# Prompt attention of a two-layer decoder step: scores of six of eight query tiles from split queries and keys, in three rounded products

## The chip, the cores and the metric

One core of a Trainium2 chip runs the whole inference step as one program. The metric is the device time of one execution in microseconds, the median of several runs. Five engines take part: TensorE (products and transposes; its weight loads have a queue of their own in the profile), VectorE, ScalarE, GpSimd and the DMA queues. Each engine works through its own instructions in the order in which they were written, and waits on semaphores where an operand comes from another engine.

## The reference, cut to what matters

The step computes two decoder layers for a prompt of 1024 tokens and eight samples of 8 tokens. The first layer's mixer is sparse attention: an indexer scores all keys for each query, the 256 best are kept, and the eight query heads (in two groups, one key head each) attend to them alone:

```python
def dsa_block(q, qi, wi, q_pos, k_all, v_all, ki_all, topk):
    ...
    _, sel = lax.top_k(score, topk)
    ...
    s = jnp.einsum('bqhgd,bqkhd->bqhgk', q, k_sel) * (HEAD_DIM ** -0.5)
    s = jnp.where(sel_valid[:, :, None, None, :], s, -jnp.inf)
    p = jax.nn.softmax(s, axis=-1)
    o = jnp.einsum('bqhgk,bqkhd->bqhgd', p, v_sel)
```

Everything is float32. What the change touches is the first `einsum`, for the prompt: head by head, 128 queries against the keys before them.

## The kernel before, in words

The program runs stage by stage: load, indexer projections, indexer scores, search of the 256th score together with the query, key and value projections, attention of the samples, **attention of the prompt** (`prompt_attention_stage`, lines 3547 to 3793), output projection, then the feed-forward, gated and second feed-forward stages, which take most of the time (702 us to the end).

The prompt attention keeps queries and keys, transposed, in `proj` (128 rows of a head by 1088 tokens; tiles `QT` to `QT + 7` are the query heads, `KTILE` and `KTILE + 1` the key heads), values in `v_nat`, and a mask per query tile in `mp`, which is 0 where a key was selected and very negative elsewhere. A query tile i has 128 queries and (i + 1) x 128 keys. The work is 64 steps, one per tile and head, in an order written out by hand: tile 0, tile 2, tile 3 (steps 0 to 23, a head at a time), then tiles 1 and 4 in turns (steps 24 to 39), then tiles 5, 6, 7 (steps 40 to 63).

A step s goes through the engines like this:

- TensorE, `scores` (line 3628): queries of the tile by the keys, in pieces of up to 512 columns, into one of two score banks. It needs `tops` of step s - 2 to be done.
- VectorE, `tops` (line 3737): adds the mask, negates, and takes the row's minimum, all in one instruction (line 3745) of the tile's whole width.
- ScalarE, `exps` (line 3690): the exponential with that minimum as bias, and the row's sum.
- VectorE: the reciprocal of the sum (line 3768).
- TensorE, `turn_probs` (line 3644): transposes the probabilities, 128 columns at a time, into two banks that ScalarE (line 3715, even groups) and VectorE (line 3764, odd groups) copy out.
- TensorE, `values` (line 3655): the product with the values; `scale_out` (ScalarE, line 3703, up to step 40, then VectorE, line 3749) divides by the sum; TensorE `turn_out` (line 3638) transposes and ScalarE `copy_out` (line 3698) writes the result over the step's queries in `proj`.

The order within one turn of the loops sets what overlaps. TensorE does `turn_probs(s)`, `values(s - 1)`, `turn_out(s - 2)`, `scores(s + 2)`. ScalarE does its copies of s, `exps(s + 1)`, `scale_out(s - 1)`, `copy_out(s - 2)`. VectorE does `tops(s + 1)`, its copies of s, the reciprocal of s, from step 41 `scale_out(s - 1)`. At the end of a turn both have other work at chosen steps: a search that lowers a threshold bit by bit for the last two tiles (`late.compare`, line 2489, on VectorE, and `late.add`, line 2496, on ScalarE, at steps 16, 18, 20, 22, 23 and every second step from 25 to 37), and the masks of tiles 4 to 7 (`masks.step`, lines 2562 to 2577, on VectorE at steps 8 to 10, 12 to 14, 40 to 42, 44 to 46; `masks.write`, line 2581, on ScalarE). From step 58 five heads' results are split for the next stage's rounded products: a copy into `hi` (line 3726) on ScalarE, and `value - hi` (line 3789) on VectorE a step later.

A float32 product appears in the trace as two matmul records with two weight loads; a transpose as one. Products of operands of type `F32R` (rounded float32) appear as one record. The other stages use such rounded products already, three in place of one: high by high, high by low, low by high. In the indexer scores it is two (lines 2939 and 2940) with the halves stacked.

The buffers of this stage lie in an arena that begins where `proj` begins, in slots of 1088 columns: `x_lo` at slot 0 lies on the query heads, `x_hi` at slot 12; slots 10 and 11 (`VTILE`) are free in this stage.

Of the kernel before, what the change touches and what calls it, by code (L numbers as in the profile page):

```python
# [20 lines left out]
F32 = mybir.dt.float32  # L21
F32R = mybir.dt.float32r
BF16 = mybir.dt.bfloat16
I32 = mybir.dt.int32
ALU = mybir.AluOpType
# [3 lines left out]
P = 128  # L29
D = 1024  # L30
KT = D // P
SEQ = 1024
# [3511 lines left out]
SPLIT_HEADS = 5  # L3544


def prompt_attention_stage(nc, proj, v_nat, Sp, level, mp, last_level, xT, x_kept, v_outs, x_parts, nxt, g):


    steps = [(i, h) for i in (0, 2, 3) for h in range(NH)]  # L3550
# [14 lines left out]
    with Scope(nc, "patt") as S:  # L3565
# [10 lines left out]
        copied = [S.sem("copied0"), S.sem("copied1")]  # L3576
        x_loaded, v_stored = S.sem("x_loaded"), S.sem("v_stored")
        hi, lo = x_parts
        out_hi, out_lo = S.sem("out_hi"), S.sem("out_lo")
        finished = {starts[7] + h + 2: h for h in range(SPLIT_HEADS)}  # L3580
        NR = len(SP_TILES)
# [44 lines left out]
        @block.tensor  # L3626
        def _(pe):
            def scores(s):
                i, h = steps[s]
                if s >= 2:  # L3630
                    pe.wait_ge(ntop_ready, s - 1)
                for a in range(0, width(s), 512):
                    w = min(512, width(s) - a)
                    last = nc.tensor.matmul(sc[s % 2][:, a:a + w], proj[:, QT + h, i * P:(i + 1) * P],
                                            proj[:, KTILE + h // GR, a:a + w], start=True, stop=True)
                last.then_inc(scored, 1)

            def turn_out(s):
                wait_scaled(pe, s)
                if s >= 1:  # L3640
                    pe.wait_ge(o_copied, s)
                nc.tensor.transpose(o_tr[:, 0:P], o_rows[:, s % 2, :], g["ident"][:, :]).then_inc(o_turned, 1)

            def turn_probs(s):
                pe.wait_ge(exp_ready, s + 1)
                for j in of_step[s]:
                    _, a, n = groups[j]
                    if j >= 2:
                        wait_copied(pe, j - 2)
                    for t in range(n):  # L3650
                        last = nc.tensor.transpose(tr[j % 2][:, t * P:(t + 1) * P], prob[:, s % 2, (a + t) * P:(a + t + 1) * P],
                                                   g["ident"][:, :])
                    last.then_inc(turned, 1)

            def values(s):
                i, h = steps[s]
                for j in of_step[s]:
                    wait_copied(pe, j)
                if s:
                    wait_scaled(pe, s - 1)  # L3660
                kv = h // GR
                for t in range(i + 1):
                    last = nc.tensor.matmul(out[:, 0:HD], probT[:, s % 2, t * P:(t + 1) * P],
                                            v_nat[:, t, kv * HD:(kv + 1) * HD], start=(t == 0), stop=(t == i))
                last.then_inc(pv_ready, 1)

            scores(0)
            scores(1)
            for s in range(n_steps):
                turn_probs(s)  # L3670
                if s:
                    values(s - 1)
                if s >= 2:
                    turn_out(s - 2)
                if s + 2 < n_steps:
                    scores(s + 2)
            values(n_steps - 1)
            for s in (n_steps - 2, n_steps - 1):
                turn_out(s)
# [9 lines left out]
        def _(act):  # L3689
# [22 lines left out]
            for s in range(n_steps):  # L3712
                for j in of_step[s]:
                    if j % 2 == 0:
                        copy_group(act, j, lambda o, i: nc.scalar.activation(o, i, ACT.Copy))
                if s + 1 < n_steps:
                    exps(s + 1)
                if 1 <= s <= by_act:
                    scale_out(s - 1)
                if s >= 2:  # L3720
                    copy_out(s - 2)
                if s in finished:
                    h = finished[s]
                    act.wait_ge(o_copied, s - 1)
                    act.wait_ge(masks.written, NR - MASKED)
                    nc.scalar.activation(hi[:, h, :], proj[:, QT + h, :], ACT.Copy).then_inc(out_hi, 1)
                if s in round_at:
                    late.add(nc, act, round_at[s])
                if s in mask_after:
                    masks.write(nc, act, mask_after[s])  # L3730
# [5 lines left out]
        def _(dve):  # L3736
# [22 lines left out]
            for s in range(n_steps):  # L3759
# [23 lines left out]
                    late.settle_level(nc, dve)  # L3783
                if s in tails:
                    masks.step(nc, dve, *tails[s])
                if s - 1 in finished:
                    h = finished[s - 1]
                    dve.wait_ge(out_hi, h + 1)
# [374 lines left out]
def trunk(nc, a, o):  # L4163
    with Scope(nc, "trunk") as T, nc.allow_non_contiguous_dma(reason="a few small vectors and 8 x 8 blocks"):
# [38 lines left out]
        with Scope(nc, "att") as A:  # L4203
# [21 lines left out]
            with Scope(nc, "masks") as C:  # L4225
# [21 lines left out]
                first = {n: Next(T, W, n, t, True, {"sgout": 1}.get(n, 2))  # L4247
                         for n, t in (("attout", attout), ("ffn0", ffn[0]), ("sgin", sgin), ("sgout", sgout), ("ffn1", ffn[1]))}
                x_parts = arena.at(T, "x_hi", [P, KT, TOK], F32R, 12), arena.at(T, "x_lo", [P, KT, TOK], F32R, 0)
                prompt_attention_stage(nc, proj, v_nat, Sp, level, mp, last_level, xT, x_kept, v_outs, x_parts, first["attout"], g)  # L4250
            ahead = [arena.at(T, f"x_ahead{i}", [P, len(AHEAD), TOK], F32R, 20) for i in range(2)]
            x_low = arena.at(T, "x_low", [P, 20, TOK], F32R, 0)
            with Scope(nc, "attoutx") as X:
# [43 lines left out]
```

## Time and profile before

| | us |
|---|---|
| median of 3 runs | 2587.63 (2586.83 to 2588.19) |
| the profiled execution, its time | 2604.05 |
| its span in the trace | 2602.3 |
| prompt attention, first score to last `copy_out` | 521.3 to 702.2 |
| busy over the span: TensorE | 2481.4 (95%) |
| VectorE | 1823.3 (70%) |
| ScalarE | 1150.1 (44%) |
| scores of the stage (line 3634): records, and time in them | 192, 77 us |

Times of instructions are those of one profiled execution. Instructions of TensorE overlap: a record lasts longer than the distance to the next one, so what a product costs is read from the distance between the starts or the ends of neighbours, not from its duration. On VectorE and ScalarE neighbours overlap by some 0.1 us. PEclk is the clock granted to TensorE, as a share of 2.4 GHz. "[0.58 <-ACT patt_prob]" at the end of a row is the engine's idle time before the instruction, and what ended it.

### The profile page before, as it was taken

The page shows a single profiled execution, that of the slowest core. Times are in us where ns is not written, and L with a number is a line of the kernel's source. Part 1 is how long each engine was busy: PE and PEld are TensorE (multiplying, and loading weights), DVE is VectorE, ACT ScalarE, POOL GpSimd, SP SyncE. Part 2 cuts the span into 40 slices and gives each one's busy share as a digit, 9 for nine tenths or more (in the row PEclk, how much of TensorE's full clock was granted, in tenths as well). Part 3 has the DMA queues.
Part 4 walks back from the last instruction along what each step waited for, and adds up shares of the span by engine and source line. Part 5 has one row for each costly group of instructions (what it writes and reads, how often), then busy time and mean ns, then how long its engine had stood idle before and what let it go on. Part 6 is the DMA issues. An engine that isn't in the chain of part 4 may idle for free. (4 is left out here: it accounts for less than half of the span.)

```text
span 2602.3 us, 49502 instructions
## 1 busy us (share of the span) xinstructions
PE 2481.4 (95%) x19001; PEld 2369.4 (91%) x19032; DVE 1823.3 (70%) x3373; ACT 1150.1 (44%) x1956; POOL 107.2 (4%) x135
## 2 busy tenths in 40 slices
PE   8899988899999999999999999989999999999898
PEld 7799955567899999999998999989999999999898
DVE  6658776777557888886575676664788888656652
ACT  5567686576534333342331353553443343323121
POOL 1310033200000000000000000000000000000000
PEclk9889999999999999999999999999999999999999
DMA  6312379820022343442775323234144433268522
GB/s 207 86 50 70 116 290 370 345 103 1 18 100 67 135 143 134 145 140 97 273 260 191 112 74 109 68 90 168 56 138 145 156 143 134 91 234 286 212 78 81
DMA packets 276591, 371.91 MB, mean 143 GB/s; under 512 B 22152, under 2 KB 215946, under 8 KB 268237
## 3 DMA queue, kind: packets, MB, share of 16 engines
q1 hardware_dynamic: 264573, 294.23, 33.2%
q0 software_dynamic: 11776, 75.50, 7.8%
q8 instruction: 101, 1.65, 0.3%
q14 instruction: 61, 0.50, 0.1%
q10 hardware_dynamic: 80, 0.02, 0.0%
HBM read 271.07 MB, written 98.63 MB: 142 GB/s over the span
## 5 line engine op out<-in xcount | busy, mean ns | idle before, releaser
L1542 PE MATMUL ffn_acc<-trunk_x_ahead,trunk_w_hi 128*128 128x272 f32 x2464 | 470.5, 290 | 5.0 <-ACT ffn_t_u L949 3.9
L1542 PE MATMUL ffn_acc<-ffn_x_later,ffn_w_hi_more 128*128 128x272 f32 x2112 | 396.4, 287 | 1.5 <-DVE trunk_xT L1190 1.5
L1542 PEld LDWEIGHTS ffn_acc<-trunk_x_ahead,trunk_w_hi 128*128 128x128 f32 x2464 | 389.0, 190 | 5.4 <-issue 5.4
L1542 PE MATMUL ffn_acc<-trunk_x_ahead,trunk_w_lo 128*128 128x272 f32 x1232 | 355.8, 289 | 0.0
L1542 PEld LDWEIGHTS ffn_acc<-ffn_x_later,ffn_w_hi_more 128*128 128x128 f32 x2112 | 330.8, 188 | 1.8 <-issue 1.8
L1542 PE MATMUL ffn_acc<-ffn_x_later,ffn_w_lo_more 128*128 128x272 f32 x1056 | 303.8, 288 | 0.0
L1542 PEld LDWEIGHTS ffn_acc<-trunk_x_ahead,trunk_w_lo 128*128 128x128 f32 x1232 | 233.7, 190 | 0.0
L1542 PEld LDWEIGHTS ffn_acc<-ffn_x_later,ffn_w_lo_more 128*128 128x128 f32 x1056 | 198.8, 188 | 0.0
L1595 PE MATMUL ffn_acc<-trunk_x_ahead,trunk_w_hi 128*128 128x272 f32 x896 | 175.2, 293 | 14.4 <-DVE trunk_xT L1415 14.1
L1595 PE MATMUL ffn_acc<-ffn_x_later,ffn_w_hi_more 128*128 128x272 f32 x768 | 149.0, 291 | 12.8 <-DVE trunk_xT L1415 6.9
L1595 PEld LDWEIGHTS ffn_acc<-trunk_x_ahead,trunk_w_hi 128*128 128x128 f32 x896 | 143.8, 193 | 15.6 <-issue 11.2
L920 ACT ACTIVATE ffn_w_hi_more<-trunk_w_raw 128x512 fp32r<-128x512 f32 x132 | 83.4, 632 | 167.8 <-PE ffn_acc L1542 163.9
L1415 DVE TENSOR_TENSOR trunk_xT<-ffn_acc,trunk_xT 128x544 f32<-128x544 f32 x136 | 98.2, 722 | 77.4 <-PE ffn_acc L1595 76.8
L920 ACT ACTIVATE trunk_w_hi<-ffn_w_sum 128x512 fp32r<-128x512 f32 x88 | 55.6, 632 | 206.7 <-DVE ffn_w_sum L1171 115.6
L1619 PE MATMUL ffn_acc<-trunk_x_ahead,trunk_w_hi 128*128 128x364 f32 (+1 forms) x576 | 141.8, 327 | 0.0
L1595 PEld LDWEIGHTS ffn_acc<-ffn_x_later,ffn_w_hi_more 128*128 128x128 f32 x768 | 122.5, 192 | 14.3 <-DVE trunk_w_lo L1404 7.7
L1595 PE MATMUL ffn_acc<-trunk_x_ahead,trunk_w_lo 128*128 128x272 f32 x448 | 130.7, 292 | 0.0
L3304 PE MATMUL search_acc<-attxm_x_pairs,attxm_w_hi 128*128 128x364 f32 (+1 forms) x480 | 122.1, 336 | 1.9 <-PEq L87 1.9
L1595 PE MATMUL ffn_acc<-ffn_x_later,ffn_w_lo_more 128*128 128x272 f32 x384 | 111.9, 291 | 0.0
L1005 ACT ACTIVATE trunk_xT<-trunk_xT 128x544 fp32r<-128x544 f32 x112 | 71.7, 655 | 90.5 <-DVE trunk_xT L1249 48.8
L1190 DVE TENSOR_TENSOR trunk_xT<-ffn_acc,ffn_u 128x544 f32<-128x544 f32 x88 | 63.6, 722 | 63.2 <-PE ffn_acc L1542 63.2
L1619 PEld LDWEIGHTS ffn_acc<-trunk_x_ahead,trunk_w_hi 128*128 128x128 f32 x576 | 101.6, 188 | 0.0
(525 smaller groups left out, 6084.6 us busy)
## 6 DMA issues: line engine op xcount, KB each, us to landing
o_kept<-trunk_xT SPq DMA_DIRECT2D x96, 544.0 KB, 5.0
trunk_w_raw<-in_ffn_w_gu SPq DMA_DIRECT2D x88, 512.0 KB, 4.0
trunk_x_ahead<-o_kept SPq DMA_DIRECT2D x56, 544.0 KB, 7.5
ffn_x_later<-o_kept SPq DMA_DIRECT2D x56, 544.0 KB, 7.6
x_saved<-trunk_xT SPq DMA_DIRECT2D x24, 544.0 KB, 2.7
trunk_w_raw<-in_ffn_w_down SPq DMA_DIRECT2D x48, 192.0 KB, 4.0
o_kept<-trunk_xT SPq DMA_DIRECT2D x32, 272.0 KB, 4.9
ffn_x_back<-x_saved SPq DMA_DIRECT2D x16, 544.0 KB, 5.8
```

The costliest lines, as they stand in the source:

```text
L920: nc.scalar.activation(w_parts(i)[0], source, ACT.Copy).then_inc(w_hi_ready, 1)
L1005: nc.scalar.activation(stage_hi[STAGE_OF[i][0]], raw_block[i], ACT.Copy).then_inc(kept_hi, 1)
L1190: nc.vector.tensor_tensor(two(out), pair(b), two(a), ALU.add).then_inc(done, 1)
L1415: nc.vector.tensor_tensor(two(out), pair(bank_of(z, n)), two(out), ALU.add).then_inc(d_added, 1)
L1542: last = nc.tensor.matmul(bank(2 * PAIR[p] + c)[:, 0:QC], w[:, k * P:(k + 1) * P], x(p, k)[:, c * QC:(c + 1) * QC], start=FRESH[p] and k = ...
L1595: last = nc.tensor.matmul(bank(2 * bank_of(z, n) + c)[:, 0:QC], w[:, k * P:(k + 1) * P], x(i, at)[:, c * QC:(c + 1) * QC], start=n in (0, ...
L1619: last = nc.tensor.matmul(bank(NC3 * (q % 2) + c)[:, 0:w], part[:, q % 2, k * P:(k + 1) * P], x[:, a:a + w], start=(k == 0 and j == 0), st ...
L3304: last = nc.tensor.matmul(banks[NC3 * (m % 2) + c][:, 0:w], part[:, k * P:(k + 1) * P], x_parts[x][:, k, a:a + w], start=(k == 0 and j == ...
```

## The change

For tiles 1, 3, 4, 5, 6 and 7 the scores are no longer one float32 product but three rounded ones into the same bank: high part of the queries by high part of the keys, high by low, low by high. Tiles 0 and 2 stay as they were.

The parts are made in this stage. A high part is a copy to type `F32R` on ScalarE, a low part is the difference to it, on VectorE. Keys are split in two halves of 512 tokens, both heads at once (128 x 2 x 512), at steps 1 and 5; the queries of a tile, all eight heads at once (128 x 8 x 128), at steps 3 (tile 3), 15 (tile 1), 17 (tile 4), 29 (tile 5), 43 (tile 6) and 47 (tile 7). Both come at the end of the step's turn on their engine, ScalarE's ahead of `late.add`, VectorE's behind `late.compare` and the masks. The low parts of the queries are written in place, over the queries; high parts have three buffers that are used in turn; `k_hi` lies in slots 10 and 11.

```diff
@@ -3544,7 +3544,7 @@
 SPLIT_HEADS = 5
 
 
-def prompt_attention_stage(nc, proj, v_nat, Sp, level, mp, last_level, xT, x_kept, v_outs, x_parts, nxt, g):
+def prompt_attention_stage(nc, proj, v_nat, Sp, level, mp, last_level, xT, x_kept, v_outs, x_parts, k_hi, nxt, g):
 
 
     steps = [(i, h) for i in (0, 2, 3) for h in range(NH)]
@@ -3576,6 +3576,14 @@
         copied = [S.sem("copied0"), S.sem("copied1")]
         x_loaded, v_stored = S.sem("x_loaded"), S.sem("v_stored")
         hi, lo = x_parts
+        split_tiles = (3, 1, 4, 5, 6, 7)
+        q_hi, k_lo = S.sb("q_hi", [P, 3, NH, P], F32R), S.sb("k_lo", [P, NKV, SEQ], F32R)
+        q_hi_ready, q_lo_ready, k_hi_ready, k_lo_ready = (S.sem(n) for n in ("q_hi_ready", "q_lo_ready", "k_hi_ready", "k_lo_ready"))
+        k_split_at, q_split_at = {1: 0, 5: 1}, {3: 0, 15: 1, 17: 2, 29: 3, 43: 4, 47: 5}
+        last_step = lambda i: max(s for s, x in enumerate(steps) if x[0] == i)
+        queries = lambda n: proj[:, QT:QT + NH, split_tiles[n] * P:(split_tiles[n] + 1) * P]
+        queries_lo = lambda n: lo[:, :, split_tiles[n] * P:(split_tiles[n] + 1) * P]
+        half_of = lambda v, e: v[:, :, 512 * e:512 * (e + 1)]
         out_hi, out_lo = S.sem("out_hi"), S.sem("out_lo")
         finished = {starts[7] + h + 2: h for h in range(SPLIT_HEADS)}
         NR = len(SP_TILES)
@@ -3629,10 +3637,21 @@
                 i, h = steps[s]
                 if s >= 2:
                     pe.wait_ge(ntop_ready, s - 1)
+                kv = h // GR
+                if i in split_tiles:
+                    n = split_tiles.index(i)
+                    pe.wait_ge(q_lo_ready, n + 1)
+                    pe.wait_ge(k_lo_ready, 1 if width(s) <= 512 else 2)
                 for a in range(0, width(s), 512):
                     w = min(512, width(s) - a)
-                    last = nc.tensor.matmul(sc[s % 2][:, a:a + w], proj[:, QT + h, i * P:(i + 1) * P],
-                                            proj[:, KTILE + h // GR, a:a + w], start=True, stop=True)
+                    if i in split_tiles:
+                        q_high, q_low = q_hi[:, n % 3, h, :], lo[:, QT + h, i * P:(i + 1) * P]
+                        for j, (q, k) in enumerate(((q_high, k_hi[:, kv, a:a + w]), (q_high, k_lo[:, kv, a:a + w]),
+                                                    (q_low, k_hi[:, kv, a:a + w]))):
+                            last = nc.tensor.matmul(sc[s % 2][:, a:a + w], q, k, start=j == 0, stop=j == 2)
+                    else:
+                        last = nc.tensor.matmul(sc[s % 2][:, a:a + w], proj[:, QT + h, i * P:(i + 1) * P],
+                                                proj[:, KTILE + kv, a:a + w], start=True, stop=True)
                 last.then_inc(scored, 1)
 
             def turn_out(s):
@@ -3719,6 +3738,14 @@
                     scale_out(s - 1)
                 if s >= 2:
                     copy_out(s - 2)
+                if s in k_split_at:
+                    e = k_split_at[s]
+                    nc.scalar.activation(half_of(k_hi, e), half_of(proj[:, KTILE:KTILE + NKV, :], e), ACT.Copy).then_inc(k_hi_ready, 1)
+                if s in q_split_at:
+                    n = q_split_at[s]
+                    if n >= 3:
+                        act.wait_ge(scored, last_step(split_tiles[n - 3]) + 1)
+                    nc.scalar.activation(q_hi[:, n % 3, :, :], queries(n), ACT.Copy).then_inc(q_hi_ready, 1)
                 if s in finished:
                     h = finished[s]
                     act.wait_ge(o_copied, s - 1)
@@ -3783,6 +3810,16 @@
                     late.settle_level(nc, dve)
                 if s in tails:
                     masks.step(nc, dve, *tails[s])
+                if s in k_split_at:
+                    e = k_split_at[s]
+                    dve.wait_ge(k_hi_ready, e + 1)
+                    nc.vector.tensor_tensor(half_of(k_lo, e), half_of(proj[:, KTILE:KTILE + NKV, :], e),
+                                            half_of(k_hi, e).bitcast(F32), ALU.subtract).then_inc(k_lo_ready, 1)
+                if s in q_split_at:
+                    n = q_split_at[s]
+                    dve.wait_ge(q_hi_ready, n + 1)
+                    nc.vector.tensor_tensor(queries_lo(n), queries(n), q_hi[:, n % 3, :, :].bitcast(F32),
+                                            ALU.subtract).then_inc(q_lo_ready, 1)
                 if s - 1 in finished:
                     h = finished[s - 1]
                     dve.wait_ge(out_hi, h + 1)
@@ -4247,7 +4284,9 @@
                 first = {n: Next(T, W, n, t, True, {"sgout": 1}.get(n, 2))
                          for n, t in (("attout", attout), ("ffn0", ffn[0]), ("sgin", sgin), ("sgout", sgout), ("ffn1", ffn[1]))}
                 x_parts = arena.at(T, "x_hi", [P, KT, TOK], F32R, 12), arena.at(T, "x_lo", [P, KT, TOK], F32R, 0)
-                prompt_attention_stage(nc, proj, v_nat, Sp, level, mp, last_level, xT, x_kept, v_outs, x_parts, first["attout"], g)
+                k_hi = arena.at(T, "k_hi", [P, NKV, TOK], F32R, VTILE)
+                prompt_attention_stage(nc, proj, v_nat, Sp, level, mp, last_level, xT, x_kept, v_outs, x_parts, k_hi, first["attout"],
+                                       g)
             ahead = [arena.at(T, f"x_ahead{i}", [P, len(AHEAD), TOK], F32R, 20) for i in range(2)]
             x_low = arena.at(T, "x_low", [P, 20, TOK], F32R, 0)
             with Scope(nc, "attoutx") as X:
```

## Rows read from the trace of the kernel before

**Rows 1.** Busy time by stretch of 15 us: PE, PEld, DVE, ACT, POOL, PEclk, DMA share, GB/s.

```profile
575.00:590.00 15.00, 13.86 (x95) 10.98 (x95) 11.15 (x41) 13.08 (x39) 0.00 (x0) 1.00 0.01 2
...
650.00:665.00 15.00, 15.00 (x103) 12.14 (x102) 8.09 (x20) 8.03 (x16) 0.00 (x0) 1.00 0.01 1
```

**Rows 2.** TensorE in order of time, tiles 6 and 7: start us, us, engine, line, operation.

```profile
656.25 1.67 PE L3634 MATMUL patt_sc<-att_proj 128*128 128x512 f32 x4
657.75 0.93 PE L3651 MATMUL patt_tr<-trunk_ident,patt_prob 128*128 128x128 f32 x7
...
660.19 1.88 PE L3634 MATMUL patt_sc<-att_proj 128*128 128x512 f32 x4
661.91 0.93 PE L3651 MATMUL patt_tr<-trunk_ident,patt_prob 128*128 128x128 f32 x7
```

**Rows 3.** TensorE in order of time, indexer scores with rounded operands, at full clock.

```profile
88.11 0.39 PE L2939 MATMUL sel_banks<-idx_k_hi,idx_q 128*128 128x512 f32 x1
...
88.58 1.00 PE L2986 MATMUL sel_banks<-att_proj 128*128 128x64 f32 x8
...
93.73 0.31 PE L2939 MATMUL sel_banks<-idx_k_hi,idx_q 128*128 128x128 f32 x1
93.88 0.27 PE L2940 MATMUL sel_banks<-idx_k_lo,idx_q 128*128 128x128 f32 x1
...
111.38 0.37 PE L2939 MATMUL sel_banks<-idx_k_hi,idx_q 128*128 128x256 f32 x1
111.59 0.28 PE L2940 MATMUL sel_banks<-idx_k_lo,idx_q 128*128 128x256 f32 x1
...
123.87 0.42 PE L2939 MATMUL sel_banks<-idx_k_hi,idx_q 128*128 128x384 f32 x1
124.13 0.34 PE L2940 MATMUL sel_banks<-idx_k_lo,idx_q 128*128 128x384 f32 x1
```

**Rows 4.** Groups of instructions by form: splits of 128x1024 elsewhere (count, busy us, mean ns).

```profile
L295 DVE TENSOR_TENSOR trunk_w_lo<-trunk_w_raw,trunk_w_hi 128x1024 fp32r<-128x1024 f32 x1 | 1.2, 1217 | 0.0
...
L291 ACT ACTIVATE trunk_w_hi<-trunk_w_raw 128x1024 fp32r<-128x1024 f32 x1 | 1.1, 1051 | 0.0
```

**Rows 5.** In order of time, all engines, tile 0 (first steps of the stage).

```profile
524.69 0.37 ACT L3708 ACTIVATE patt_o_rows<-patt_out,patt_rtotal 128x128 f32<-128x128 f32 x1 [0.60 <-PE patt_out L3663]
...
525.12 0.29 DVE L3745 CUSTOM_DVE_ANT_0 patt_prob<-patt_sc,masks_mp 128x128 f32<-128x128 f32 x1 [0.49 <-PE patt_sc L3634]
...
527.63 0.27 ACT L3701 ACTIVATE att_proj<-patt_o_tr 128x128 f32<-128x128 f32 x1
527.67 0.29 DVE L3745 CUSTOM_DVE_ANT_0 patt_prob<-patt_sc,masks_mp 128x128 f32<-128x128 f32 x1 [0.45 <-PE patt_sc L3634]
```

**Rows 6.** Busy time by stretch of 1 us, start of the stage.

```profile
524.00:525.00 1.00, 1.00 (x6) 0.89 (x5) 0.36 (x2) 0.40 (x2) 0.00 (x0) 0.50 1.08 304
```

**Rows 7.** In order of time, steps 14 to 18, tile 2 into tile 3.

```profile
548.60 0.69 DVE L3745 CUSTOM_DVE_ANT_0 patt_prob<-patt_sc,masks_mp 128x512 f32<-128x512 f32 x1 [0.33 <-PE patt_sc L3634]
...
548.87 0.26 ACT L3701 ACTIVATE att_proj<-patt_o_tr 128x128 f32<-128x128 f32 x1
...
550.90 0.60 PE L3651 MATMUL patt_tr<-trunk_ident,patt_prob 128*128 128x128 f32 x4
...
553.40 0.69 DVE L3745 CUSTOM_DVE_ANT_0 patt_prob<-patt_sc,masks_mp 128x512 f32<-128x512 f32 x1 [0.93 <-PE patt_sc L3634]
```

**Rows 8.** In order of time, tiles 1 and 4, around step 29.

```profile
581.93 0.82 DVE L3745 CUSTOM_DVE_ANT_0 patt_prob<-patt_sc,masks_mp 128x640 f32<-128x640 f32 x1
...
583.76 0.77 PE L3651 MATMUL patt_tr<-trunk_ident,patt_prob 128*128 128x128 f32 x5 [0.58 <-ACT patt_prob L3695]
```

**Rows 9.** In order of time, tile 5 and the start of tile 6.

```profile
619.78 0.27 ACT L3701 ACTIVATE att_proj<-patt_o_tr 128x128 f32<-128x128 f32 x1
...
620.11 0.96 DVE L3745 CUSTOM_DVE_ANT_0 patt_prob<-patt_sc,masks_mp 128x768 f32<-128x768 f32 x1 [1.05 <-PE patt_sc L3634]
...
634.20 1.09 DVE L3745 CUSTOM_DVE_ANT_0 patt_prob<-patt_sc,masks_mp 128x896 f32<-128x896 f32 x1 [0.92 <-PE patt_sc L3634]
```

## The prediction

> **What bounds the kernel now.** The change touches one stage, the prompt attention, 521.3 to 702 us of the trace. I read first how busy each engine is by stretch, to see who could be the limit. In the long tiles TensorE has no free time and the other two are little over half busy [rows 1]; where tiles 1 and 4 alternate, TensorE has over 1 us free in 15 while ScalarE is busy 13.1 of 15 [rows 1]. So there are two kinds of stretch: TensorE-bound ones (most of tile 3, the end of tile 5, tiles 6 and 7), where cheaper scores are time, and ones bound by a loop through VectorE (`tops`), ScalarE (`exps`) and TensorE (turning the probabilities), where they are not. Next I read TensorE in order of time for what scores cost [rows 2], and the indexer's scores, the nearest work with rounded operands [rows 3]; last, ScalarE and VectorE in order of time at the eight steps where splits are put in [rows 5, 7, 8, 9].
>
> **Scores.** A full-precision product shows as two records. In tile 7 the scores (2 x 512 columns) start at 660.19 and the next transposes at 661.91: 1.72 us, 0.86 per 512 columns. In tile 6 (512 + 384) it is 1.50 us, so 0.64 for 384 [rows 2]; at the same rate per column 256 cost 0.43 and 128 cost 0.215. A rounded pass is one record. Two of 512 columns take 88.11 to 88.58, 0.235 each; 384, by the ends (124.29 and 124.47), 0.18; 256 (111.75 and 111.87) 0.12; 128 (94.04 and 94.15) 0.11 [rows 3]. Three passes: 0.70, 0.54, 0.36, 0.33. So 512 columns save 0.16, 384 save 0.10, 256 save 0.07, and 128 *lose* 0.11, since a pass that short is as long as its weight load. Per step: tile 7 0.32, tile 6 0.26, tile 5 0.23, tile 3 0.16, tile 1 0.07, tile 4 0.05; times 8 heads, 8.7 us of TensorE time in all. TensorE's clock is full in both groups of rows.
>
> The rows say 0.70 against 0.86, which is 0.82. The Trainium skill (FP8 and Floating Point Precision, TensorE Precision Notes) says that true FP32 takes four passes through the array; three for four would be 0.75, 0.65 us for 512 columns, and 8 x (0.43 + 0.38 + 0.32 + 0.27 + 0.22 + 0.11), some 13.8 us, instead of 8.7. The rows decide, and no run here yet shows these three passes themselves.
>
> **What of it reaches the end.** Tiles 1 and 4: nothing. TensorE waits for an exponential before each tile-4 step (0.58 us at 583.76 [rows 8]), and its own scores are not in that loop. Tile 3: TensorE sets the pace there from step 17 to 22; of the five scores in between, the first two fall before the second of my stalls below, so 3 x 0.16 = 0.5. Tile 5: VectorE is full there with the masks of tiles 6 and 7, and one step's 0.2 counts. Tiles 6 and 7: five steps x 0.26 and eight x 0.32, 3.9. Together **-4.6 us**.
>
> **The splits.** Eight pairs: two for the keys (steps 1, 5), six for queries (3, 15, 17, 29, 43, 47). Each is a 128x1024 copy on ScalarE and a 128x1024 subtraction on VectorE; the nearest rows are 1.05 and 1.22 us [rows 4]. In work that is 8.4 and 9.8 us on engines with time to spare. But the order decides. In a step, ScalarE does the exponential of step s+1, the scaling, the copy out, and then the rounding; VectorE waits for it at the end of the same step, and behind that wait stands `tops` of s+2, for which the next exponential waits, and for that TensorE. So `tops` starts at ScalarE's end of the step + 1.05 + 1.22 instead of when its scores are there.
> - Step 1: ScalarE is done at 524.69 + 0.37 = 525.06, so the subtraction ends at 527.33; `tops` began at 525.12 [rows 5]: 2.2 late. TensorE, at half clock there [rows 6], was a few tenths behind; I take 1.7.
> - Step 3: done at 527.90, so 530.17 against 527.67 [rows 5]: 2.5, with nothing to hide it.
> - Step 5: the same pattern, 2.2. Scores that TensorE does meanwhile give back 0.5. Tile 0 together: +5.9.
> - Step 15: done at 549.13, so 551.40 against 548.60: 2.8. Then 1.6 for `tops` and exponential: 553.0, against TensorE's next turn at 550.90 [rows 7]. I take +2.0.
> - Step 17: all is 2.0 later by now, and ScalarE also does one of the search's additions every second step, so that I estimate the end of its step at 555.7. With 2.3 for the pair `tops`, at 553.40 before [rows 7], comes at 558.0: 4.6 late, 2.6 more than what came over from step 15, of which I take 0.6 for TensorE's margin. Another +2.0.
> - Step 29: VectorE is full until 581.93 [rows 8], by when the copy is done; only the 1.2 of the subtraction count, and TensorE waited there already: +1.2.
> - Steps 43, 47: ScalarE is done with 43 at 619.78 + 0.27 = 620.05, so the subtraction ends at 622.3 against 620.11, where VectorE had waited 1.05 for scores [rows 9]: 2.2 late, of which about 1.2 stay, since VectorE's masks of the next steps leave it no other gap. At 47 the same comes on top: `tops`, at 634.20 before [rows 9], would start at 637.9, 3.7 late. In a step of 3.94 us (656.25 to 660.19 [rows 2]) `tops` (1.09) and the exponential (some 1.2) leave TensorE 1.7 of margin: together +2.0.
>
> Sum: 5.9 + 2.0 + 2.0 + 1.2 + 2.0 = **+13.1 us**. Bounds of each: 0 if the engine ahead has the slack, and the full 2.3 of the pair of instructions. The waits that the change gives TensorE (low parts ready) are met many steps before. The wait for a query buffer at 29, 43 and 47 is for scores of steps 23, 38 and 39, done by then. No DMA is added or moved.
>
> **The clock.** TensorE's granted clock is 0.50 (the 1.2 GHz level) at 524 [rows 6], after the thin work between the two stages. With three stalls of some 2 us in tile 0 TensorE is again thinly used, and I expect part of tiles 0 and 2 at the lower level. A step of tile 0 has six 128-column records of 0.11, 0.66 us at full clock; about half of them lie in the loop, so half clock costs some 0.3 us a step. Five steps of that: **+1.5**. Bounds: nothing, and 4 us if the first steps of tile 2, with three times the products, also run at half clock.
>
> **Sum.** -4.6 + 13.1 + 1.5 = +10.0. The profiled execution took 2604.05 us (span 2602.3), 0.6% over the median of 2587.63; the differences are in microseconds of one stage and carry over: 2614 for a profiled execution, **2597** for the median (I shade the sum down by half a microsecond, since every stall was taken alone). The stage behind starts from TensorE's last transposes, so what is lost here stays lost. A measurement of this kernel can tell about 0.2%, 5.2 us.
>
> **Rivals.**
> - *Faster: the stalls are hidden.* If the copy and the subtraction slip into idle time what is left is TensorE's gain on the TensorE-bound steps: 5 x 0.16, 6 x 0.23, 8 x 0.26 and 8 x 0.32, 6.8 in all, so 2581. For: in tiles 6 and 7 both engines have 7 of 15 us free [rows 1]. Against: only two of the eight splits come near those tiles, and rows 5 and 7 show `tops` starting as soon as its scores are there, so that whatever stands before it is late work. It decides if `tops` behind a split starts less than 0.5 us late. 0.14.
> - *No change: half hidden.* The stalls of tile 0 shrink because engines run ahead in the gaps, steps 43 and 47 are absorbed by TensorE's margin, and the clock is as before: 3 + 3 + 1 - 5 = +2, 2590. 0.25.
> - *Slower by more: the clock.* If TensorE stays at half clock from 524 through the first steps of tile 2, 1.5 becomes 4 to 5 and stalls add to each other: 2601. For: the fall at 524 after thin work. Against: it was back within some 3 us. It decides at the granted clock of 530 to 540. 0.15, beside 0.46 for the forecast itself; both are slower, 0.61.
> - *The change doesn't do what it says:* if a rounded pass issued as two records, scores would cost half more. The 44 rounded indexer products have 44 records, so under 0.01.
>
> **Numbers.** Faster by over 0.2% (below 2582.4) 0.14; within 0.25; slower (above 2592.8) 0.61. Range 2583 to 2603: the lower end leaves out the fully hidden case, the upper end is the bad clock with full stalls.
>
> **What the profile after would show.** (1) Scores of tile 7 take about 1.40 us before the transposes, not 1.72; one record per pass. (2) Behind each of steps 1, 3, 5, 15 and 17, VectorE idle for about 1 us waiting for ScalarE's rounding copy, then TensorE idle about 2 us for an exponential. (3) Tile 0 takes about 15 us, not 9. (4) No gain in tiles 1 and 4; tiles 6 and 7 4 us shorter. (5) A granted clock of 0.5 within 527 to 540. I am wrong if VectorE's wait for the copy is short, if the transposes behind a split don't wait, or if the passes interleave to less than 0.23 us for 512 columns.

## The result, and the profile after

| | before | after |
|---|---|---|
| median of 9 runs each, one chip, us | 2588.19 (2586.83 to 2594.66) | 2596.61 (2591.68 to 2600.47) |
| ratio, 95% interval | | 1.003 (1.002 to 1.0041) |
| prompt attention, first score to the first product of the output projection, us | 181.2 | 190.3 |
| where that stage starts in the trace, us | 521.3 | 507.3 |

The kernel is slower by 8.4 us. The forecast was 2597 on a median of 2587.63, 9.4 more; its sum was +10.0. The profiled execution after is shorter in all (2593.72 us, span 2591.9) than the one before: its prompt attention starts 14 us earlier, since the stages ahead of it, which the change doesn't touch, took less time in that execution. So everything below compares the stage alone: 190.3 against 181.2, 9.1 us longer.

To see where, take the first transposes of each step, counted from those of step 0, in both traces. The difference is the delay that the change has built up by that step (us; the other columns are the experiments below):

| step | after | E1 | E2 | E3 | E4 | E5 | E6 | E8 |
|---|---|---|---|---|---|---|---|---|
| 3 | 1.65 | -0.09 | 1.65 | -0.01 | 0.07 | -0.01 | 1.65 | 0.00 |
| 5 | 4.11 | 1.06 | 4.12 | 0.45 | 1.04 | 0.45 | 3.81 | 0.00 |
| 7 | 6.37 | 2.02 | 6.38 | 0.57 | 1.55 | 0.58 | 5.77 | 0.00 |
| 16 | 6.39 | 2.39 | 6.40 | 0.58 | 1.58 | 3.96 | 5.79 | 0.00 |
| 17 | 8.33 | 2.80 | 8.34 | 0.48 | 1.99 | 3.86 | 7.73 | -0.09 |
| 19 | 10.07 | 3.02 | 10.08 | 0.33 | 2.20 | 3.72 | 9.47 | -0.24 |
| 25 | 9.86 | 3.13 | 10.16 | -0.11 | 1.91 | 5.50 | 9.27 | -0.68 |
| 33 | 11.28 | 3.50 | 11.59 | -0.10 | 2.00 | 5.50 | 11.39 | -0.61 |
| 40 | 11.29 | 3.51 | 11.61 | -0.08 | 2.04 | 7.91 | 11.36 | -0.53 |
| 49 | 13.06 | 4.12 | 13.63 | -0.61 | 1.50 | 9.43 | 13.14 | -1.04 |
| 56 | 11.08 | 2.07 | 13.68 | -2.66 | -0.54 | 7.39 | 11.14 | -3.08 |
| 63 | 9.13 | 0.10 | 13.69 | -4.62 | -2.50 | 5.44 | 9.20 | -5.05 |

All engines in order of time, tile 0 of the kernel after, steps 1 and 3 (rows of other lines left out). These answer to [rows 5].

```profile
510.93 1.05 ACT L3743 ACTIVATE trunk_k_hi<-att_proj 128x1024 fp32r<-128x1024 f32 x1
...
512.01 1.23 DVE L3816 TENSOR_TENSOR patt_k_lo<-att_proj,trunk_k_hi 128x1024 fp32r<-128x1024 f32 x1 [1.41 <-ACT trunk_k_hi L3743]
...
513.15 0.28 DVE L3772 CUSTOM_DVE_ANT_0 patt_prob<-patt_sc,masks_mp 128x128 f32<-128x128 f32 x1
...
514.03 0.47 PE L3670 MATMUL patt_tr<-trunk_ident,patt_prob 128*128 128x128 f32 x1 [1.45 <-ACT patt_prob L3714]
...
515.59 1.06 ACT L3748 ACTIVATE patt_q_hi<-att_proj 128x1024 fp32r<-128x1024 f32 x1
...
516.68 1.23 DVE L3821 TENSOR_TENSOR trunk_x_lo<-att_proj,patt_q_hi 128x1024 fp32r<-128x1024 f32 x1 [1.78 <-ACT patt_q_hi L3748]
...
518.70 0.48 PE L3670 MATMUL patt_tr<-trunk_ident,patt_prob 128*128 128x128 f32 x1 [1.60 <-ACT patt_prob L3714]
```

Read it as one chain: VectorE idles 1.41 us until ScalarE's copy is done, subtracts for 1.2, and only then does `tops` (513.15), whose scores were there some 2 us before; the exponential follows, and TensorE has idled 1.45 us when it comes. The same chain at steps 15 and 29, where [rows 7] and [rows 8] were:

```profile
541.39 1.05 ACT L3748 ACTIVATE patt_q_hi<-att_proj 128x1024 fp32r<-128x1024 f32 x1
542.48 1.23 DVE L3821 TENSOR_TENSOR trunk_x_lo<-att_proj,patt_q_hi 128x1024 fp32r<-128x1024 f32 x1 [1.83 <-ACT patt_q_hi L3748]
...
545.21 0.66 PE L3670 MATMUL patt_tr<-trunk_ident,patt_prob 128*128 128x128 f32 x4 [1.94 <-ACT patt_prob L3714]
...
576.61 1.06 ACT L3748 ACTIVATE patt_q_hi<-att_proj 128x1024 fp32r<-128x1024 f32 x1
...
577.76 1.22 DVE L3821 TENSOR_TENSOR trunk_x_lo<-att_proj,patt_q_hi 128x1024 fp32r<-128x1024 f32 x1
...
580.73 0.77 PE L3670 MATMUL patt_tr<-trunk_ident,patt_prob 128*128 128x128 f32 x5 [1.87 <-ACT patt_prob L3714]
```

At step 29 the subtraction has no bracket: VectorE was full until 577.8, and the copy had ended at 577.67, just in time. Over the stage, the waits sum up so (line waited for: us, times, longest):

```profile
PE patt_tr L3670 <- ACT patt_prob L3714: 20.4, 24, 1.9
DVE patt_prob L3772 <- PE patt_sc L3651: 13.2, 15, 1.3
...
DVE trunk_x_lo L3821 <- ACT patt_q_hi L3748: 9.8, 5, 2.1
...
DVE patt_k_lo L3816 <- ACT trunk_k_hi L3743: 3.2, 2, 1.8
```

TensorE waited for an exponential 6.8 us in the stage before (14 times) and now 20.4. VectorE waits 13.0 us for copies, seven times (at step 29 it doesn't), and correspondingly less for scores: 13.2 us for rounded ones and 2.1 for float32 ones, where it had been 29.7. Its wait changed its place from ahead of a `tops` whose scores weren't there to ahead of one whose scores were.

TensorE in order of time, scores of tile 7 after, answering to [rows 2]:

```profile
667.06 1.03 PE L3670 MATMUL patt_tr<-trunk_ident,patt_prob 128*128 128x128 f32 x8
...
669.75 0.48 PE L3651 MATMUL patt_sc<-trunk_k_hi,patt_q_hi 128*128 128x512 f32 x1
670.07 0.40 PE L3651 MATMUL patt_sc<-patt_k_lo,patt_q_hi 128*128 128x512 f32 x1
670.31 0.40 PE L3651 MATMUL patt_sc<-trunk_k_hi,trunk_x_lo 128*128 128x512 f32 x1
670.54 0.39 PE L3651 MATMUL patt_sc<-trunk_k_hi,patt_q_hi 128*128 128x512 f32 x1
670.77 0.39 PE L3651 MATMUL patt_sc<-patt_k_lo,patt_q_hi 128*128 128x512 f32 x1
671.00 0.39 PE L3651 MATMUL patt_sc<-trunk_k_hi,trunk_x_lo 128*128 128x512 f32 x1
671.23 1.03 PE L3670 MATMUL patt_tr<-trunk_ident,patt_prob 128*128 128x128 f32 x8
```

One record per pass, and from 670.07 to 671.23 five passes in 1.16 us, 0.232 each, so six take 1.39. The first starts 0.32 ahead of the second, in the shadow of a transpose that began at 669.72. The step is 671.23 - 667.06 = 4.17 us; the same step before was 4.49.

Busy time by stretch of 1 us at the start of the stage (PE, PEld, DVE, ACT, POOL, PEclk, DMA share, GB/s), answering to [rows 6]:

```profile
509.00:510.00 1.00, 0.48 (x4) 0.29 (x4) 0.30 (x2) 0.98 (x5) 0.00 (x0) 0.56 1.08 314
...
517.00:518.00 1.00, 0.09 (x1) 0.00 (x0) 1.00 (x2) 0.00 (x0) 0.00 (x0) 0.50 1.00 405
...
522.00:523.00 1.00, 0.62 (x1) 0.00 (x0) 1.00 (x5) 0.17 (x1) 0.00 (x0) 0.61 1.02 402
523.00:524.00 1.00, 0.62 (x3) 0.46 (x4) 0.58 (x4) 1.00 (x5) 0.00 (x0) 1.00 1.05 376
```

The granted clock is 0.50 (1.2 GHz) in every microsecond between. By the shares in the first and the last of them it stood there for 13.7 us, from 1.8 to 15.5 us into the stage; before, for 3.4 us, from 2.5 to 5.9 us into it. VectorE alone at work for a whole microsecond (517) is the stall.

### The profile page after: what moved, and what is told of

It reads as the page before. It is cut to its first block and busy times, and to the rows that moved or that the text cites. A ratio compares the mean times of both kernels' runs of the same rounds, so it can differ in the third digit from the quotient of the medians.

```text
span 2591.9 us, 49730 instructions
## 1 busy us (share of the span) xinstructions
PE 2466.5 (95%) x19081; PEld 2374.9 (92%) x19112; DVE 1829.7 (71%) x3381; ACT 1156.9 (45%) x1964; POOL 108.2 (4%) x135
## 5 line engine op out<-in xcount | busy, mean ns | idle before, releaser
L1595 PEld LDWEIGHTS ffn_acc<-trunk_x_ahead,trunk_w_hi 128*128 128x128 f32 x896 | 143.0, 192 | 17.6 <-issue 13.2
```

Of the source, the lines that this page charges most:

```text
L1595: last = nc.tensor.matmul(bank(2 * bank_of(z, n) + c)[:, 0:QC], w[:, k * P:(k + 1) * P], x(i, at)[:, c * QC:(c + 1) * QC], start=n in (0, ...
```

## Experiments

The theory after this: the eight pairs cost 13.7 us (the 9.1, and the 4.6 that the passes were to give), and they cost it as *waits in a fixed order* (copy, subtraction, then `tops`), hardly as work; the passes give 4.6; the low clock adds something. Rivals: the work itself is what costs; the passes give more or less than their share in the last tiles; the clock is most of tile 0. Diffs are against the changed kernel.

**E1, the subtraction a step later.** The same work, but VectorE no longer waits for a copy of its own step.

```diff
-                if s in k_split_at:
-                    e = k_split_at[s]
+                if s - 1 in k_split_at:
+                    e = k_split_at[s - 1]
...
-                if s in q_split_at:
-                    n = q_split_at[s]
+                if s - 1 in q_split_at:
+                    n = q_split_at[s - 1]
```

> Each of the eight subtractions moved one step later on VectorE, nothing else changed. The stage (first score to the first product of the output projection) took 181.2 us before and 190.3 after the change. Order theory (VectorE's wait for ScalarE's copy holds up tops): the wait goes, ScalarE's 1.05 and VectorE's 1.2 stay but now lie beside each other's slack; each split costs about 1.2 instead of 1.2 to 2.1, tile 0 is 3 to 3.5 us longer than before instead of 6.2, the stage 184 to 186, the kernel 2590 to 2593. Work theory (the copies and subtractions cost what they are long, wherever they stand): the stage stays at 189.5 to 190.5, the kernel at 2596 to 2597.

Measured: 2587.16 us (2584.13 to 2590.17, 11 runs), kernel before on that chip 2589.35; ratio 0.9993 (0.9983 to 1.0003). The stage took 181.3 us, 0.1 more than before the change and 2.7 below the lower end of what I expected. In order of time, step 3:

```profile
513.15 1.05 ACT L3748 ACTIVATE patt_q_hi<-att_proj 128x1024 fp32r<-128x1024 f32 x1
...
514.24 1.23 DVE L3821 TENSOR_TENSOR trunk_x_lo<-att_proj,patt_q_hi 128x1024 fp32r<-128x1024 f32 x1 [0.82 <-ACT patt_q_hi L3748]
514.80 0.33 PE L3670 MATMUL patt_tr<-trunk_ident,patt_prob 128*128 128x128 f32 x1 [0.78 <-ACT patt_prob L3714]
...
515.38 0.28 DVE L3772 CUSTOM_DVE_ANT_0 patt_prob<-patt_sc,masks_mp 128x128 f32<-128x128 f32 x1
```

The copy runs while VectorE does the `tops` that the next exponential needs; `tops` after next waits instead, which is less urgent. All of the change's loss is gone with the same instructions: 9.1 - 0.1 = 9.0 us were order. That includes what the order did to the clock, which was at 0.50 for only 3.4 us here, as before the change; E6 below puts a price on it. At step 49 the column stands at 4.1: what the work of the splits costs (2.4 in tile 0, where a step is shorter than the pair), less the little that the passes gave until there. In tiles 6 and 7 the passes give 4.0 back. At steps 15 and 17 the pairs cost 0.6 together instead of 3.7.

**E2, the splits alone.** All eight pairs stay, and every score is one float32 product again (with the low part of the queries, which lies where they were; their values are left out).

```diff
-                if i in split_tiles:
+                if i in ():
...
-                        last = nc.tensor.matmul(sc[s % 2][:, a:a + w], proj[:, QT + h, i * P:(i + 1) * P],
+                        q = lo[:, QT + h, i * P:(i + 1) * P].bitcast(F32) if i in split_tiles else proj[:, QT + h, i * P:(i + 1) * P]
+                        last = nc.tensor.matmul(sc[s % 2][:, a:a + w], q,
```

> All splits as in the changed kernel, but the scores are one float32 product as before (for the six tiles with the low part of the queries, so their values are left out). If the passes give what the rows said (4.6 us on the path), the stage is 190.3 + 4.9 = 195 us and the kernel 2601; if the passes give nothing and the splits cost 9, the stage is 190 to 191 and the kernel 2597.

Measured: 2602.74 us (5 runs), ratio 1.0052 (1.0039 to 1.0065); the stage 194.9. The E2 column follows that of after to step 19 and then lacks only what the passes give: 0.3 at 25, 0.6 at 49, and 13.69 - 9.13 = 4.6 at the end. From step 25 to 40 both columns rise by 1.4, so in tiles 1 and 4 the passes gave nothing.

**E3, the passes alone.** No splits; the parts are buffers of zeros, filled by GpSimd at the start, so queries and keys are left out of these scores.

```diff
+        @block.gpsimd
+        def _(pool):
+            for t in (q_hi[:, :, :, :], k_lo[:, :, :], k_hi[:, :, :]):
+                nc.gpsimd.memset(t.bitcast(F32), 0.0).then_inc(q_lo_ready, 1)
...
-                    pe.wait_ge(q_lo_ready, n + 1)
+                    pe.wait_ge(q_lo_ready, 3)
...
-                        q_high, q_low = q_hi[:, n % 3, h, :], lo[:, QT + h, i * P:(i + 1) * P]
+                        q_high = q_low = q_hi[:, n % 3, h, :]
```

> Three rounded passes, no splits: the parts are zeroed once by GpSimd and the masks alone then decide (the split of queries and keys is left out). My sum: TensorE's gain on its own steps, 5 to 7 us: stage 174 to 176, kernel 2581 to 2583. If a pass is dearer than in the indexer's rows: stage 178 or more.

Measured: 2582.87 us (7 runs), ratio 0.9975 (0.9964 to 0.9985); the stage 176.5, 4.6 under the kernel before and 0.5 over the upper end of what I expected from it. Its column has 0.57 at step 7, where no score has changed yet: the granted clock was 0.50 for 6.8 us here, not 3.4. In E8, whose first steps are the same for TensorE, it was 3.4 and the column shows 0.00, so the 0.57 is the clock's. Behind that E3's column falls by 0.7 to step 25, by 0.5 from 40 to 49 and by 4.0 in tiles 6 and 7. E2 and E3 add up, 13.7 - 4.6 = 9.1, but in part by luck: the 4.6 is 5.2 of passes less 0.6 of clock, and alone the passes give 0.7 in tile 3 where beside the splits they gave 0.3.

**E5, both parts on GpSimd.** The copy and the subtraction leave ScalarE and VectorE altogether.

```diff
+        @block.gpsimd
+        def _(pool):
...
+                    nc.gpsimd.tensor_copy(q_hi[:, n % 3, :, :], queries(n)).then_inc(q_hi_ready, 1)
...
+                    nc.gpsimd.tensor_tensor(queries_lo(n), queries(n), q_hi[:, n % 3, :, :].bitcast(F32),
+                                            ALU.subtract).then_inc(q_lo_ready, 1)
```

> Copy and subtraction of all eight splits on GpSimd, at the same steps' semaphores but with no place in ScalarE's and VectorE's order. Order theory and work theory both: what they lose is given back unless GpSimd is late or slows VectorE: stage 174 to 177, kernel 2581 to 2584. Rival: GpSimd takes so long for 128x1024 (over 5 us for a pair) that the first scores of tile 3 wait, or VectorE's instructions get longer beside it: stage 180 or more.

Measured: 2591.06 us (12 runs), ratio 1.0006 (0.9997 to 1.0015); the stage 186.6, ten more than my theory allowed: the rival was right. GpSimd and VectorE in order of time:

```profile
523.33 0.78 DVE L2564 TENSOR_SCALAR patt_tail_eq<-masks_Sp,masks_level 128x640 bf16<-128x640 f32 x1
...
523.85 2.50 POOL L3649 TENSOR_TENSOR trunk_x_lo<-att_proj,patt_q_hi 128x1024 fp32r<-128x1024 f32 x1
...
525.10 2.59 DVE L2570 TENSOR_TENSOR_SCAN patt_rank<-patt_tail_eq 128x640 f32<-128x640 bf16 x1
...
526.30 2.23 POOL L3647 CAST patt_q_hi<-att_proj 128x1024 fp32r<-128x1024 f32 x1
...
528.61 2.81 POOL L3649 TENSOR_TENSOR trunk_x_lo<-att_proj,patt_q_hi 128x1024 fp32r<-128x1024 f32 x1
...
529.24 2.52 DVE L2577 TENSOR_TENSOR patt_tail_hit<-patt_tail_hit,patt_tail_eq 128x640 bf16<-128x640 bf16 x1
...
556.00 2.37 POOL L3649 TENSOR_TENSOR trunk_x_lo<-att_proj,patt_q_hi 128x1024 fp32r<-128x1024 f32 x1
...
556.17 2.22 DVE L2512 SCALAR_TENSOR_TENSOR masks_last_level<-masks_last_level,patt_late_drop 128x2 int32<-128x2 int32 x1
...
558.42 1.15 ACT L2496 ACTIVATE patt_late_hit<-masks_Sp,masks_last_level 128x1024 bf16<-128x1024 f32 x1 [1.38 <-DVE masks_last_level L2512]
```

A VectorE instruction of two numbers a partition takes 2.22 us and ends at 558.39, when GpSimd's subtraction ends (558.37); undisturbed it is 0.16. The mask's sum takes 2.52, to the end of GpSimd's at 531.4 and its own 0.49 less an overlap. It works the other way too: GpSimd's copy, 1.04 elsewhere, takes 2.23 and ends 0.84 behind VectorE's scan. `tops`, which reads its scores from PSUM, and the copies out of PSUM kept their times, which is why the pairs in tile 0 cost nothing (E5 and E3 are equal to step 7). Two inputs in SBUF are no condition, though: the mask's comparison (line 2564), with one, took 0.78 and not 0.55, and one of the search's on two numbers (line 2510), also with one, 0.95 and not 0.17. The delay comes at once from step 8 to 16 (+3.4) and between 19 and 25 (+1.8), with the masks and the search. Of the +3.9 between 33 and 49 the search accounts for 2.3, at step 39. The next 1.8 came at step 41 with GpSimd at rest: TensorE had stood idle for 2.4 us ahead of step 39, and from 600.9 to 607.7 its granted clock was 0.50. The Trainium skill (SBUF — State Buffer, Who interferes with whom) says that VectorE and GpSimd share one pair of SBUF ports, that it is an exclusive lock, and that a VectorE instruction with two SBUF inputs contends with a GpSimd instruction that reads SBUF; the times above agree with that.

**E6, TensorE kept busy in tile 0.** Three 128-column products ahead of the transposes of steps 2 to 7, in an unused part of a score bank.

```diff
+                if 2 <= s < 8:
+                    for _ in range(3):
+                        nc.tensor.matmul(sc[0][:, 512:512 + P], g["ident"][:, :], g["ident"][:, :], start=True, stop=True)
```

> The changed kernel, with three float32 products of 128 columns (six records, 0.66 us at full clock) that nobody reads put ahead of each step's transposes in steps 2 to 7, into a score bank that is free then. After the change TensorE's clock stood at 0.50 for 13 us (509.5 to 522.5). If that clock costs what I had put down for it (1.5 us), it comes back some us earlier here and the eighth step's transposes come at 6.2 - 1 to 6.2 + 0.5 us beyond before (the products themselves lie in the stalls); the 2.2 us of each split stay. If the clock, not VectorE's order, were the cause of tile 0's 6.2 us, they would fall to 3 or less.

Measured: one execution, 2601.43 us; the stage 190.4, that of after 190.3. Stretches of 1 us, same columns as above:

```profile
515.00:516.00 1.00, 1.00 (x7) 1.00 (x6) 0.42 (x1) 0.55 (x1) 0.00 (x0) 0.50 1.27 319
516.00:517.00 1.00, 1.00 (x8) 1.00 (x8) 1.00 (x4) 0.28 (x1) 0.00 (x0) 0.65 1.02 379
517.00:518.00 1.00, 0.98 (x9) 0.72 (x7) 0.38 (x6) 0.95 (x5) 0.00 (x0) 1.00 1.01 399
```

The clock was back at 516.7, 5.9 us into the stage, as before the change, where after it had taken 15.5. Yet tile 0 was only 0.6 us shorter (5.77 against 6.37 at step 7). So the low clock for some 10 us more is worth about 0.6 us of 6.4, net of what the added products cost (0.1 at step 4); the waits are the rest. E6 lost those 0.6 again between steps 25 and 33 (+2.1 against +1.4), and the clock took them too:

```profile
585.00:586.00 1.00, 1.00 (x4) 0.80 (x3) 0.82 (x4) 1.00 (x6) 0.00 (x0) 0.50 0.03 8
...
588.00:589.00 1.00, 1.00 (x9) 1.00 (x9) 0.00 (x0) 0.64 (x2) 0.00 (x0) 0.81 0.00 0
```

It stood at 0.50 from 585.0 to 588.4; it fell 1.3 us after the end of TensorE's wait of 1.9 us at step 31, while in the kernel after, behind the same wait, it stayed at full. Between the transposes of steps 31 and 32 that cost 0.75 us.

**E4, the subtraction on GpSimd, the copy on ScalarE.**

```diff
+        @block.gpsimd
+        def _(pool):
...
+                    pool.wait_ge(q_hi_ready, n + 1)
+                    nc.gpsimd.tensor_tensor(queries_lo(n), queries(n), q_hi[:, n % 3, :, :].bitcast(F32),
+                                            ALU.subtract).then_inc(q_lo_ready, 1)
```

> ScalarE's copies where they are, only the subtractions moved to GpSimd. There a 128x1024 subtraction took 2.35 us, and VectorE's bf16 sum for a mask took 2.5 us beside it, not 0.5, and its scan 2.6, not 1.5. Theory (VectorE and GpSimd shut each other out for some operations): where a GpSimd subtraction meets VectorE's masks or the small instructions of the search (steps 17, 29, 43), 1 to 2 us are lost; elsewhere only ScalarE's 1.05 counts, under 0.8 each. Tile 0: 2 to 3 us; the stage 182 to 185, the kernel 2589 to 2592. If the slow VectorE instructions in the other run had another cause, the stage is 180 to 181.

Measured: 2591.26 us (10 runs), before on that chip 2594.89; ratio 0.9985 (0.9976 to 0.9994); the stage 178.7, so my expectation was some 3 to 6 us too high. Groups of VectorE in this kernel, with mean ns, show why:

```profile
L2512 DVE SCALAR_TENSOR_TENSOR masks_last_level<-masks_last_level,patt_late_drop 128x2 int32<-128x2 int32 x12 | 2.0, 163 | 0.4
...
L2577 DVE TENSOR_TENSOR patt_tail_hit<-patt_tail_hit,patt_tail_eq 128x640 bf16<-128x640 bf16 x1 | 0.5, 492 | 0.0
```

The same two as in E5, at their undisturbed 0.16 and 0.49: with the subtraction tied to the step of the copy, no instruction that E5 had drawn out met GpSimd. Four others did, three of the search's comparisons (line 2489) and one of a mask's (line 2562), which have one input in SBUF and sum up, and they kept their 1.13 to 1.15 and 1.27 us. The expectation had 180 to 181 for "another cause", and the stage came out below that too, so E4 by itself doesn't decide; E5's rows do. ScalarE's copies cost 1.55 by step 7 and 0.6 at steps 15 and 17, next to nothing later.

**E8, what the runs advise.** Tiles 1 and 4 keep float32 products (nothing to gain there); the two key halves and tile 3's queries are split by GpSimd, which must be done before the masks' first scan; the other three pairs are at 29, 33 and 47 with the subtraction a step late.

```diff
-        split_tiles = (3, 1, 4, 5, 6, 7)
+        split_tiles = (3, 5, 6, 7)
...
-        k_split_at, q_split_at = {1: 0, 5: 1}, {3: 0, 15: 1, 17: 2, 29: 3, 43: 4, 47: 5}
+        k_split_at, q_split_at = {}, {29: 1, 33: 2, 47: 3}
...
+            for part, n in (("k", 0), ("q", 0), ("k", 1)):
...
+                nc.gpsimd.tensor_copy(high, whole).then_inc(a, 1)
+                pool.wait_ge(a, n + 1)
+                nc.gpsimd.tensor_tensor(low, whole, high.bitcast(F32), ALU.subtract).then_inc(b, 1)
```

> Three passes for tiles 3, 5, 6 and 7 alone; keys and tile 3's queries split on GpSimd in tile 0, where it ran beside VectorE without cost; tiles 5, 6 and 7 on ScalarE at steps 29, 33 and 47 and on VectorE a step later. Order theory: no stall in tile 0, 0.4 each at 29 and 33, none at 47, the whole gain of 4.6 in tiles 3, 5, 6 and 7 (tiles 1 and 4 gave nothing): stage 177 to 178 us, kernel 2584 to 2586, faster than both. If tiles 1 and 4 had given something after all: 178.5 or more. Work theory: four queries and two keys cost as before, stage 184 or more.

Measured: 2591.60 us (2588.22 to 2600.40, 11 runs), before on that chip 2594.89; ratio 0.9987 (0.9977 to 0.9997). The stage took 176.1, 5.0 less than before, 14.2 less than after, and 0.9 below what I expected. GpSimd's last subtraction ends at 527.5, and VectorE's first scan starts at 529.19, with its usual 1.48:

```profile
517.18 1.04 POOL L3641 CAST trunk_k_hi<-att_proj 128x1024 fp32r<-128x1024 f32 x1 [12.40 <-issue]
518.30 2.36 POOL L3643 TENSOR_TENSOR patt_k_lo<-att_proj,trunk_k_hi 128x1024 fp32r<-128x1024 f32 x1
...
525.14 2.37 POOL L3643 TENSOR_TENSOR patt_k_lo<-att_proj,trunk_k_hi 128x1024 fp32r<-128x1024 f32 x1
...
529.19 1.48 DVE L2570 TENSOR_TENSOR_SCAN patt_rank<-patt_tail_eq 128x640 f32<-128x640 bf16 x1
```

Beside E3's column, E8's rises by 0.1 at most at a split, and it ends where the passes alone end (-5.05, E3 -4.62 with its 0.57 of clock). By the stage it beats both kernels. By whole runs it is 3.3 us under the kernel before, with an interval that just excludes no change; the kernel after, in its own set of runs, was 8.4 over it.

## Why the prediction was right, step by step

| term | predicted | measured (column "after") |
|---|---|---|
| tile 0: steps 1, 3, 5 | +5.9 | 6.4 at step 7 less 0.6 of clock (E6): +5.8 |
| clock | +1.5 | +0.6 (E6, net of its added products) |
| step 15 | +2.0 | 8.33 - 6.39: +1.9 |
| step 17 | +2.0 | 10.07 - 8.33: +1.7 |
| tile 3 | -0.5 | 9.86 - 10.07: -0.2 |
| step 29 | +1.2 | 11.28 - 9.86: +1.4 |
| tile 5 and steps 43, 47 | -0.2 + 2.0 | 13.06 - 11.29: +1.8 |
| tiles 6 and 7 | -3.9 | 9.13 - 13.06: -3.9 |
| sum | +10.0 | +9.1 |

- *The order decides.* That VectorE's wait stands ahead of `tops`, and `tops` ahead of the next exponential, was the main step, and it held at each place; E1 shows it, since its edit changes nothing but the order (the shorter stretch of low clock follows from that). It held more strictly than I had it afterwards: I expected E1 to keep 3 to 5 us of loss, and it kept 0.1.
- *The clock* is the term that was mis-sized. The fall came where I put it (the 0.50 stretch lies 1.8 to 15.5 us into the stage) and lasted until 0.6 us ahead of step 7's transposes. "Half clock costs some 0.3 us a step" is about right for steps that don't stall: E3, with 3.4 us more of it, was 0.19 later at step 4, 0.46 at step 5 and 0.57 from step 7 on. It was wrong for stalled ones: TensorE is idle there for 0.8 to 1.6 us anyway, and I read the small price as its slower products fitting into that time. E6 measured 0.6 for some 10 us. The clock's rival (4 to 5 us) falls with it, although its condition, half clock for long, was nearly met. Where TensorE sets the pace the same clock is dear: 1.8 us in tile 5 in E5.
- *Both sums, E2's and E3's.* The pairs were put at 13.1 + 1.5 and cost 13.7; the passes were put at 4.6 and gave 4.6 beside the splits (E2's column less that of after). The single stalls were rougher than their sum: several had been taken between bounds, such as the 0.5 given back in tile 0. In after, tile 3 gave 0.2 and not 0.5, while steps 43 and 47 with tile 5 came out at 1.8 as forecast, though E2 splits that into +2.0 of pairs and -0.2 of passes (13.63 - 11.61 = 2.02).
- *Passes by rows, not by the page.* A rounded pass of 512 columns was 0.232 to 0.233 us, against 0.235 read from [rows 3], so three are 0.70 and float32 is 0.86. The Trainium skill (FP8 and Floating Point Precision, TensorE Precision Notes) says that true FP32 takes four passes; three of four would make it 0.65, an estimate from that count. The measured 0.70 is 0.81 of the 0.86.
- *The points to look for.* Point 1 came out (1.39 us for six passes). In point 2, VectorE's waits are 1.4 to 2.1 us each, not about 1: they begin when VectorE itself runs out of work, which is earlier than I drew it; the delay was reckoned from ScalarE's end and so stayed right. TensorE waited 1.4 and 1.6 us behind steps 1 and 3, 1.9 and 1.7 behind 15 and 17, and 0.75 behind step 5, where tile 2's longer scores filled part of it; I had said about 2. Point 3: tile 0 is 6.4 us longer. Point 4 held (E2's and after's columns rise alike in tiles 1 and 4). Point 5 held, nearly to the end of tile 0.
- *The rivals.* "The stalls are hidden" would have been true with the subtraction a step later and the first splits elsewhere: 2581 was forecast for it, and E8 is 5.0 us under the kernel before by the stage, where that rival had 6.8. "Half hidden" had 2590; nothing was hidden in the kernel as it is.

## What to carry to other kernels

When an engine must wait for another's result within one turn of a loop, look at what stands behind the wait in its order, and who waits for that: two instructions with 2.3 us of work cost 1 to 2.5 us of the whole kernel each time, and the same instructions with the subtraction a turn later cost between nothing (step 47) and 1.1 (step 43, among the masks), E1's column beside E3's. Before work is put on GpSimd, look at which VectorE instructions with inputs in SBUF run beside it, those with two above all. Beside `tops` and the copies from PSUM it cost nothing here; put beside the masks and the search it made the stage 10 us longer than the passes alone (E5), where VectorE's own subtraction a turn late made it 4.7 longer (E1). Replace a float32 product by three rounded ones where TensorE sets the pace and the columns are many; here 13 of the 48 steps with three passes brought 3.9 of the 4.6 us.

## What the hardware showed unexpectedly

- VectorE and GpSimd held each other off for whole instructions: 0.49 became 2.52, 1.48 became 2.59 and 0.16 became 2.22 us on VectorE, and 1.04 became 2.23 on GpSimd. Instructions that read PSUM were untouched, and so were the comparisons that sum up; two with one input in SBUF were not (0.55 to 0.78, 0.17 to 0.95).
- GpSimd copies 128x1024 in 1.04 us, as fast as ScalarE's 1.05, but subtracts it in 2.36, twice VectorE's 1.23.
- GpSimd's first instruction came 2.2 us into the stage in all three kernels in which it waits for nothing (517.18 in E8, 512.48 in E5, 507.26 in E3), with an idle time of some 12.4 us ahead of it that no wait of the profile explains.
- The price of the half clock depends on who sets the pace: some 10 us more of it cost 0.6 us in stalled steps (E6), 3.4 us more cost 0.57 in the same steps unstalled (E3), and 6.8 us cost 1.8 in tile 5 (E5).
- How long the clock stayed low differed between executions with the same work for TensorE: 3.4 us at the start of the stage in E8, 6.8 in E3 and E5.
- In nine profiled executions the stage started anywhere from 505.1 to 521.3 us though nothing ahead of it differed, more than the whole effect under study. Only a comparison inside the stage could carry the terms.
